# The opening phase of a one-core hybrid block: tokens turned by diagonal products, modulation weights loaded in groups, first projection weights kept

## The reference, cut to what matters

```python
mod_x = silu(c) @ w_ada + b_ada              # latent; six pieces of 1024 columns
mod_c = silu(c_ctx) @ w_ada + b_ada          # context
hx = rmsnorm(x, norm1_g) * (1 + sc1x) + sh1x
hc = rmsnorm(ctx, norm1_g) * (1 + sc1c) + sh1c
p  = h @ w_in                                # then two groups of mixers, merge, w_out, squared-ReLU MLP
```

## Time and profile before

| | us |
|---|---|
| median of 3 runs | 1781.2 |
| lowest and highest | 1779.32 and 1784.86 |
| profiled execution, its own time | 1786.23 |
| its span | 1784.4 |
| end of the last instruction of `modulate_phase` | 67.17 |
| first projection product | 74.98 |

### The profile page before, as it was taken

One profiled execution on the slowest core, in us unless ns is written; L12 is line 12 of the kernel. 1 busy time (PEld: TensorE's weight loads), 2 busy tenths in 40 slices (PEclk: granted clock), 3 DMA queues, 4 the chain that ended last, 5 costly groups with the idle time before them and its releaser, 6 DMA issues. The chain is left out here.

```text
span 1784.4 us, 35206 instructions
## 1 busy us (share of the span) xinstructions
PE 1579.5 (89%) x15022; PEld 1331.5 (75%) x15022; DVE 1015.5 (57%) x1542; ACT 640.9 (36%) x976; POOL 420.3 (24%) x369
## 2 busy tenths in 40 slices
PE   4599999999987878888876798799999989899997
PEld 1366887899987777777775687578888867787886
DVE  2534553101105777767676655845545588887975
ACT  3367436212112232222222323445545543233333
POOL 1301111111103555545544220422222200000000
PEclk7699999999998999989899899999999999999998
DMA  7213324336545433333322232044444487163422
GB/s 309 76 47 104 108 91 124 102 114 185 169 127 136 133 109 108 109 109 109 108 62 84 93 115 95 24 130 141 163 151 144 161 314 253 54 235 115 168 83 95
DMA packets 170269, 229.94 MB, mean 129 GB/s; under 512 B 34205, under 2 KB 102049, under 8 KB 169090
## 3 DMA queue, kind: packets, MB, share of 16 engines
q1 hardware_dynamic: 163602, 206.85, 35.9%
q0 software_dynamic: 6512, 20.84, 3.7%
HBM read 165.91 MB, written 61.73 MB: 128 GB/s over the span
## 5 line engine op out<-in xcount | busy, mean ns | idle before, releaser
L87 PE MATMUL fps<-xh_m,w1r_hi 128*128 128x512 f32 x448 | 177.5, 396 | 19.2 <-ACT s L2373 5.4
L87 PE MATMUL fps<-bh,ah 128*128 128x512 f32 x448 | 176.5, 394 | 14.3 <-DVE acc L2688 9.8
L88 PE MATMUL fps<-xl_m,w1r_hi 128*128 128x512 f32 x448 | 176.7, 394 | 0.0
L89 PE MATMUL fps<-xh_m,w1r_lo 128*128 128x512 f32 x448 | 176.4, 394 | 0.0
L89 PE MATMUL fps<-bh,al 128*128 128x512 f32 x448 | 175.7, 392 | 0.0
L88 PE MATMUL fps<-bl,ah 128*128 128x512 f32 x448 | 175.7, 392 | 0.0
L80 PE MATMUL ps_main<-hhi,whi 128*128 128x512 f32 (+3 forms) x360 | 137.0, 381 | 15.6 <-DVE wlo L694 11.7
L81 PE MATMUL ps_main<-hlo,whi 128*128 128x512 f32 (+3 forms) x360 | 133.5, 371 | 0.0
L82 PE MATMUL ps_main<-hhi,wlo 128*128 128x512 f32 (+3 forms) x360 | 133.4, 371 | 0.0
L2335 ACT ACTIVATE ah<-araw 128x2048 fp32r<-128x2048 f32 x28 | 53.7, 1918 | 186.0 <-PE fps L89 120.0
L80 PE MATMUL ps_main<-whi,hhi 128*128 128x256 f32 x416 | 120.2, 289 | 0.0
(11 more groups left out here) (304 smaller groups left out, 3575.0 us busy)
## 6 DMA issues: line engine op xcount, KB each, us to landing
s_hid<-hb SPq DMA_DIRECT2D x112, 256.0 KB, 2.3
araw<-s_hid SPq DMA_DIRECT2D x28, 1024.0 KB, 6.6
w1raw<-in_w_ff SPq DMA_DIRECT2D x16, 1024.0 KB, 6.2
w2b<-in_w_ff SPq DMA_DIRECT2D x16, 1024.0 KB, 6.9
raw<-in_w_in SPq DMA_DIRECT2D x14, 1024.0 KB, 5.3
wa<-in_w_ada SPq DMA_DIRECT2D x8, 1024.0 KB, 10.5
z_sb<-in_w_ada SPq DMA_DIRECT2D x16, 512.0 KB, 4.3
n_sb<-in_w_ada SPq DMA_DIRECT2D x16, 512.0 KB, 4.3
```

What stands on the lines that cost most here:

```text
L87: pe.matmul(out, lhi, rhi, start=start, stop=False, skip_group_check=True)
L88: pe.matmul(out, lhi, rlo, start=False, stop=False, skip_group_check=True)
L89: return pe.matmul(out, llo, rhi, start=False, stop=stop, skip_group_check=True)
```

## The change

In `modulate_phase`, a tile's `rstd` no longer multiplies the tokens. DVE multiplies the identity by it (a 128x128 diagonal, `diag`), and PE multiplies the token tile by this diagonal, an fp32 product that turns and scales at once, eight for a tile. What comes out is copied to `xt`, by DVE for tiles 0 to 5 and by ACT for 6 to 9. W_ada is loaded in five groups of feature columns (`GROUPS`: 2, 2, 2, 1 and 1 blocks of 128, shift and scale), the first between token tiles 5 and 6, the third to fifth into the memory of token tiles that have been turned. After each group comes a small chain of its own: `columns` (PE), `row` (ACT), `select` (PE), `scales` (DVE), and then for its feature blocks scale and shift in place (`full`, DVE or ACT), rounding (`high`, ACT) and subtraction (`low`, DVE) over 512 to 1280 tokens at a time. POOL has no part in it any more. The weights of "small" are loaded at the end of the phase's SP queue and split at the end of ACT's and DVE's, into tiles that both phases see (`K.ws_hi`, `K.ws_lo`). In `project_phase`, the "small" load and split are gone, the "k" weights are the first load, and the first product waits for nothing. Two small buffers move into the memory of others.

```diff
@@ modulate_phase @@
+        GROUPS = ((0, 2), (2, 2), (4, 2), (6, 1), (7, 1))
+        TOGETHER = ((0, 1), (1, 1), (2, 2), (4, 2), (6, 2), (8, 2))
+        xt = m.sb("xturn", [P, KT, NTOK])
+        junk = K.hhi[:, KT - 1, :D]
+        wa = m.sb("wa", [P, 2, 4 * D])
+        wslot = [x.rearrange("p (z k n) -> p z k n", z=2, k=KT) for x in
+                 (wa[:, 0], wa[:, 1], *(xs[:, a:b].rearrange("p t d -> p (t d)") for a, b in ((0, 4), (4, 6), (6, 8))))]
...
+        diag = K.gt2[:, 512:1024].rearrange("p (x n) -> p x n", n=P)
...
+        PIECES = [(0, 0, HALF), (1, 0, HALF), (0, HALF, NTOK), (1, HALF, NTOK), (2, 0, NTOK), (3, 0, NTOK), (4, 0, NTOK),
+                  (5, 0, NTOK), (6, 0, NTOK), (7, 0, HALF), (7, HALF, NTOK)]
+        BY_ACT = (1, 3, 5, 6)
+        T_ACT = 6
...
+            def load_w(g):
+                k, n = GROUPS[g]
+                for z in range(2):
+                    sp.dma_start(wslot[g][:, z], wv[:, z, :, k * P:(k + n) * P]).then_inc(ld_w[g][z], 16)
+
+            for t in range(4, 6):
+                sp.dma_start(xs[:, t], xr[t]).then_inc(ld_x[t], 16)
+            load_w(0)
+            for t in range(6, NT):
+                sp.dma_start(xs[:, t], xr[t]).then_inc(ld_x[t], 16)
+            load_w(1)
+            for g, last in ((2, 3), (3, 5), (4, 7)):
+                sp.wait_ge(t_ready, 2 * last + 2)
+                load_w(g)
+            wi = A["w_in"].rearrange("(k p) n -> p k n", p=P)
+            sp.wait_ge(wpad_done, 1)
+            sp.dma_start(wraw[:, :, 0:16], wi[:, :, OFF_R:OFF_R + 16]).then_inc(ld_small, 16)
+            sp.dma_start(wraw[:, :, 32:48], wi[:, :, OFF_AB:OFF_AB + 16]).then_inc(ld_small, 16)
...
+            def turned(t):
+                for h in range(2):
+                    act.wait_ge(t_ready, 2 * t + h + 1)
+                    act.activation(xt[:, features(h), tokens(t)], ps_t[:, 2 * (t % 2) + h].rearrange("p (k n) -> p k n", n=P),
+                                   ACT.Copy).then_inc(t_act, 1)
+
+            def row(g):
+                n = GROUPS[g][1]
+                act.wait_ge(w_used, g + 1)
+                if g:
+                    act.wait_ge(mod_ready, g)
+                act.activation(modrow[:, :2 * n * P], ps_row[:, :2 * n * P], ACT.Copy).then_inc(row_done, 1)
+
+            def full(x):
+                k, lo, hi = PIECES[x]
+                act.wait_ge(sc1_done, [k in range(a, a + n) for a, n in GROUPS].index(True) + 1)
+                if hi > HALF:
+                    act.wait_ge(t_act, 2 * (NT - T_ACT))
+                act.wait_ge(t_dve, 2 * T_ACT)
+                full_piece(act, lambda a, s, b: act.activation(a, a, ACT.Identity, scale=s, bias=b), x, hf_act)
+
+            def high(x):
+                k, lo, hi = PIECES[x]
+                act.wait_ge(hf_act if k in BY_ACT else hf_dve, fulls(x))
+                act.activation(K.hhi[:, k, lo:hi], xt[:, k, lo:hi], ACT.Copy).then_inc(hi_done, 1)
...
+                for t in range(t0, t0 + n):
+                    if t >= 4:
+                        dve.wait_ge(t_ready, 2 * (t - 3))
+                    dve.tensor_scalar(diag[:, t % 4], K.ident[:], rstd[:, t:t + 1], None, ALU.mult).then_inc(diag_done, 1)
+
+            def turned(t):
+                for h in range(2):
+                    dve.wait_ge(t_ready, 2 * t + h + 1)
+                    dve.tensor_copy(xt[:, features(h), tokens(t)],
+                                    ps_t[:, 2 * (t % 2) + h].rearrange("p (k n) -> p k n", n=P)).then_inc(t_dve, 1)
...
+            def turn(t):
+                pe.wait_ge(diag_done, t + 1)
+                if t >= 2:
+                    pe.wait_ge(t_dve, 2 * min(t - 1, T_ACT))
+                if t - 2 >= T_ACT:
+                    pe.wait_ge(t_act, 2 * (t - 1 - T_ACT))
+                for h in range(2):
+                    for i in range(4):
+                        k = 4 * h + i
+                        last = pe.matmul(ps_t[:, 2 * (t % 2) + h, i * P:(i + 1) * P], xs[:, t, k * P:(k + 1) * P],
+                                         diag[:, t % 4], start=True, stop=True)
+                    last.then_inc(t_ready, 1)
+
+            def columns(g):
+                n = GROUPS[g][1] * P
+                if g:
+                    pe.wait_ge(row_done, g)
+                for z in range(2):
+                    pe.wait_ge(ld_w[g][z], 16)
+                    for k in range(KT):
+                        q = slice(32 * (k % 4), 32 * (k % 4) + 32)
+                        last = pe.matmul(ps_row[q, z * n:(z + 1) * n], K.csil[:, k, :], wslot[g][:, z, k], start=(k < 4),
+                                         stop=(k >= 4))
+                last.then_inc(w_used, 1)
+
+            def select(g):
+                n = GROUPS[g][1]
+                pe.wait_ge(row_done, g + 1)
+                if g == 0:
+                    pe.wait_ge(sel_done, 1)
+                if g == 1:
+                    pe.wait_ge(cols_done, 1)
+                if g >= 2:
+                    pe.wait_ge(mod_done, g - 1)
+                for i in range(2 * n):
+                    last = pe.matmul(both[g % 2][:, 8 * g + 2 * i:8 * g + 2 * i + 2], modrow[:, i * P:(i + 1) * P], sel2[:],
+                                     start=True, stop=True)
+                last.then_inc(mod_ready, 1)
...
@@ project_phase, PE @@
-            pe.wait_ge(init_done, 3)
...
-                pe.wait_ge(lo_done, u + 1)
+                if u:
+                    pe.wait_ge(lo_done, u)
...
-                        last = mm3(pe, ps_main[:width, i % 3, :n], whi[:, b, k, :width], wlo[:, b, k, :width],
+                        last = mm3(pe, ps_main[:width, i % 3, :n], K.ws_hi[:, k], K.ws_lo[:, k],
```

More of the change, by code:

```diff
@@ new lines, in high, with roots @@
+            def high(x):
+                k, lo, hi = PIECES[x]
+                act.wait_ge(hf_act if k in BY_ACT else hf_dve, fulls(x))
+                act.activation(K.hhi[:, k, lo:hi], xt[:, k, lo:hi], ACT.Copy).then_inc(hi_done, 1)
+            def roots(r):
+                t, n = TOGETHER[r]
+                square(t)
+                if n == 2:
+                    square(t + 1)
+                rsqrt(r)
+            for r in range(5):
+                roots(r)
+            row(0)
+            roots(5)
@@ new lines, in _ @@
+            turned(6)
+            full(1)
+            turned(7)
+            high(0)
+            high(1)
+            turned(8)
+            turned(9)
+            full(3)
+            high(2)
+            high(3)
+            row(1)
+            full(5)
+            high(4)
+            high(5)
+            row(2)
+            full(7)
+            high(6)
+            high(7)
+            row(3)
+            full(8)
+            high(8)
+            act.wait_ge(ss_done, NT)
+            row(4)
@@ L202, in _ @@
+            high(9)
+            high(10)
+            act.wait_ge(ld_small, 32)
+            act.activation(K.ws_hi[:], wraw[:], ACT.Copy).then_inc(small_hi, 1)
         @block.vector
@@ L254, in _ @@
-            if on_dve(len(units) - 1):
-                low(len(units) - 1)
+            scales(0)
+            full(0)
+            variance(5)
+            diagonal(5)
+            low(0)
+            low(1)
+            full(2)
+            low(2)
+            low(3)
+            scales(1)
+            full(4)
+            low(4)
+            low(5)
+            scales(2)
+            full(6)
+            low(6)
+            low(7)
+            scales(3)
+            low(8)
+            scales(4)
@@ L283, in _ @@
[L283 to L296 removed]
+            columns(0)
@@ L299, in project_phase @@
+            select(0)
+            turn(6)
+            turn(7)
+            turn(8)
+            turn(9)
+            for g in range(1, NG):
+                columns(g)
+                select(g)
 def project_phase(nc, A, K, S):
```

278 lines of the change are left out of this document (124 added, 154 removed).

## The result

| | before | changed kernel |
|---|---|---|
| median | 1781.05 us (4 executions) | 1765.15 us (4 executions) |
| lowest and highest | 1779.32 and 1784.86 | 1763.3 and 1768.08 |
| profiled execution, its own time | 1786.23 | 1768.08 |
| its span | 1784.4 | 1766.3 |
| first projection product | 74.98 | 62.94 |

The ratio is 0.9906, with a 95% interval of 0.9884 to 0.9927. The direction was right, the size too small.

A forecast was written before the change was run, and what follows sets the result against it. PE's long run bounds the kernel, so its first product sets the end. The chain summed to a start at 66.1 against 74.98 us: gain 8.9, 1781.2 to 1772.3 us, range 1766.5 to 1780.5.

The forecast's parts named there:

- step 2: PE turns six token tiles by diagonal products: three half tiles at 2.01 us, nine at 1.09, ending at 23.7 us.
- steps 5 and 6: Group 1's columns at 1.2 GHz, to 40.8 us; then ACT-paced rounds of groups 1 to 3, to 60.0 us.
- steps 3 and 4: Group 0's columns, row and select, to 27.5 us; then turning four tiles at 8 x 1.09 us, to 36.2.
- rivals C and D: C (0.08): products never raise PE's clock, 1790.8 us. D (0.05): a later wait takes back the earlier start, about 1781.
- rival B: Chain losses: hand-overs 1.1 us, durations 3.9, clock falling at 30 us 4.6; time 1776 to 1781 us; chance 0.19.
- rival A: PE stays at or near 2.4 GHz to the phase's end: gain 12.1 us, time 1769 us; chance 0.18.
- Step 7: Tail of the first phase: last select, scales, full, high, low and small weights' split, ending at 65.1 us.

The follow-up runs named there:

- small weights kept alone: Kernel before, with only the small unit's weights loaded and split in its first phase, and the changed projection phase: median 1774.48 us, ratio 0.9969.
- new opening alone: Changed kernel with the small weights loaded and split behind the barrier again, as in the kernel before: median 1775.54 us, ratio 0.9964.
- changed, late start: Changed kernel with its first token load held back by ten POOL memsets: median 1777.57 us, ratio 0.9985.
- changed, second trace: Changed kernel run again without edits, beside the kernel before: median 1766.22 us, ratio 0.9912.
- rows early: Changed kernel with each group's ACT row moved ahead of the two roundings, and DVE's scales ahead of the second subtraction: median 1761.11 us, ratio 0.9895.
- tail on POOL: Kernel with rows early, plus one tail subtraction on POOL and the small weights' split in an earlier gap: median 1765.09 us, ratio 0.9911.
- small split in the gap: Kernel with rows early, plus the small weights' split in gaps of ACT and DVE, all subtractions on DVE: median 1762.71 us, ratio 0.9881.
- first group behind the tokens: Changed kernel with the first W_ada group loaded behind all ten token tiles: 1775.77 us, one execution.
- transposes: Changed kernel with plain transposes in place of the diagonal products, tokens not normalised by their own root: 1765.0 us, one execution.
- 24 filling products: Small split in the gap, plus unused PE products between columns and select of groups 1 to 4 and 24 behind the last select: 1762.05 us, ratio 0.9878.
- 14 filling products: Version with 24 filling products, with 14 instead of 24 behind the last select: median 1757.57 us, ratio 0.9878.

## Why the prediction was right, and where it was wrong

The forecast was 1772.3 us, and 1765.15 was measured. Of the 7.15 us between them, 3.2 are in the opening (first product at 62.94, not 66.1): the largest term is step 2, the price of the diagonal product, with 2.05 us, and next steps 5 and 6, with 1.9, where a low clock was taken for work that went at the high one (steps 3 and 4 were 0.8 us too short). The other 4 us are in no step, and their cause stays open.

**The bound and the barrier: right.** Whatever moves PE's first product moves the end. Against the gain by medians of the same sessions (two versions have one execution only):

| kernel | first product | earlier by | faster by | behind |
|---|---|---|---|---|
| small weights kept alone | 68.85 | 6.1 | 6.1 | 1711.3 |
| new opening alone | 67.34 | 7.6 | 5.1 | 1711.4 |
| changed, late start | 73.45 | 1.5 | 3.1 | 1699.1 |
| changed, first trace | 62.94 | 12.0 | 15.9 | 1703.4 |
| changed, second trace | 60.18 | 14.8 | 13.9 | 1703.9 |
| rows early | 58.09 | 16.9 | 19.5 | 1699.9 |
| tail on POOL | 60.07 | 14.9 | 15.0 | 1702.4 |
| small split in the gap | 60.31 | 14.7 | 18.9 | 1701.2 |
| first group behind the tokens (1) | 67.86 | 7.1 | 4.3 | 1706.1 |
| transposes (1) | 61.59 | 13.4 | 15.1 | 1701.6 |
| 24 filling products | 58.34 | 16.6 | 19.5 | 1701.0 |
| 14 filling products | 58.15 | 16.8 | 22.5 | 1697.7 |

The differences between the third and the fourth column go both ways, from -2.8 to +5.7 us; in the last two rows some 2 us are the faster small unit. One column is of one execution, the other a median of several. So rivals C and D are out: the start is kept, and the products raised the clock, as the window from 14 to 20 us shows (PE busy throughout, 1.00):

```profile
14.00:20.00 6.00, 6.00 (x55) 5.94 (x55) 4.88 (x11) 1.56 (x4) 0.00 (x0) 1.00 1.09 366
```

**Kept small weights: right.** 6.9 us of waiting behind the barrier were to go. From the phase's last instruction to the first product it is 7.9 us without the kept weights and 1.05 with them, 6.9 less.

**Step 2, the price of the diagonal product: wrong, and the largest error.** I took 2.01 and 1.09 us for half a tile from the earlier trace rows. The run of four tiles in the second trace, all at 2.4 GHz, gives 7.39/8 = 0.92 us for half a tile. The single records say it for both clocks: eight starts 0.213 us apart are 1.71 us at 1.2 GHz, eight 0.111 apart are 0.89 at 2.4. In the first trace the distance changes at 13.3 us, so 27 records of the first six tiles went at the one and 69 at the other: 5.8 + 7.7 = 13.4 us, and 0.5 us was spent where a run or a group begins. Together that is the measured 21.40 - 7.45 = 13.95 us. The forecast had 16.0, so the step was 2.05 us too long, of the 3.2 by which the first product was forecast too late. The earlier trace rows are differences between starts of two groups, and the single records of the same trace show what that adds: in the group at 540.56 the first two starts stand 0.38 us apart, the next ones 0.21, and 0.35 lie between the last and the group behind. That is 0.30 us in 2.01 which a long run pays once and not for each half tile; in the other group it is 0.20 in 1.09.

**Steps 3 and 4: too short by 0.8 us.** ACT's row came late for select 0 (1.51 us of wait in front of it; 4.36 us for the step, not 3.8), and the clock fell in step 4 (8.95, not 8.7), where with the clock up it would have been 7.3. In the second trace it was. This is rival B's falling clock in one execution and not in the other; it cost 1.6 us where B had 4.6.

**Steps 5 and 6: the clock did not fall at 36 us.** The granted clock was still up there, in the view of windows 1.00 from 36 to 40:

```profile
36.00:40.00 4.00, 1.84 (x24) 1.26 (x20) 2.25 (x4) 2.75 (x5) 0.00 (x0) 1.00 1.16 298
...
41.00:62.00 21.00, 9.24 (x96) 6.78 (x88) 13.00 (x21) 13.29 (x17) 0.00 (x0) 0.50 0.17 32
```

So the columns of group 1 took 1.93 us and not 3.86, and the second select 1.05 and not 1.88. Step 5 took 4.1 and not 4.6 us; it gained less than its columns because ACT's row stood only at 38.18, so ACT set the pace one step earlier than forecast. The rounds took 6.1, 6.7 and 5.1 us instead of 7.2, 6.95 and 5.05. This is the front half of rival A; the back half did not come, for from 41 to 62 us the clock was at 0.50 (second row). The form of the rounds was right: ACT sets the pace, with a gap ended by DVE's scales in each. Their `full` was dearer than the 1.47 us I took (1.73), the gaps up to 0.9 us shorter than 2.4 (1.5, 2.35, 1.8). **Step 7** was right: 5.3 us for 5.1.

With the chain's true length the forecast would have been 1781.2 - 12.0 = 1769.2, rival A's time, inside the range. **The last 4 us** are in no step. Behind the first product PE's instructions are the same in the two kernels (the order of a few loads differs), and still the four traces with the old opening or the old small unit have 1707.8 to 1711.4 us there, the ten others 1697.7 to 1706.1. Two things in the runs go with that. The four were taken of executions 3 to 7.4 us above the median of their kernel (that of the kept weights was the slowest of its twelve), and of the others the changed kernel's first was 2.9 us above, the rest 0.6 at most (two have a single execution). With that taken off, more than half of the difference is gone. And the clock stood at 1.2 GHz for 127 to 151 us behind the first product in the four, and for 111 to 126 in the ten; the spread is mostly between 600 and 1000 us. The first trace of before had 129, the changed kernel's 120: 9 us at half the clock are at most 5 us of work, an estimate. Why the clock was low for longer there no run shows. The late start, with the whole change in it, had 119.

Executions of the kernel before ran from 1772.88 to 1799.47 us with nothing changed. Over the 62 executions beside these experiments the mean is 1781.3, over the ten of the changed kernel 1766.1: 15.2 us, against 12.0 and 14.8 from the two traces' first products. What is left, some 2 us, these runs don't tell from the scatter, and whether there is a lasting part stays open. The forecast failed here in that its range had no term for this scatter: two medians of four executions drawn from those 62, whose standard deviation is 4.5 us, differ by 3 us or so without a cause in the code. That is an estimate.

The fastest versions are the three with early rows and the small split in the gap or with filling, 1757.6 to 1762.7 us, and the one with early rows alone at 1761.1. All have medians below the changed kernel's 1765.15 and 1766.22, but the intervals of their ratios overlap with its own. Which of them is best is not resolved.

## What to carry to other kernels

Where one engine runs almost without a gap behind a barrier, find its first instruction in the trace and measure changes ahead of it by that place: where the clock ahead of it was the same, it showed within one execution what eight executions blurred. Price a repeated instruction from a long run of its own kind (its time over the count of its records), not from the difference between starts of two short groups. And in a chain of engines, put what another engine waits for ahead of one's own long work; that was worth 2 us of path here for moving eight lines.

## What was unexpected of the hardware

The granted clock fell in the midst of work without a gap. In the version with 24 filling products PE was never idle from 50 to 57 us, and yet (columns as in the earlier trace rows):

```profile
50.00:51.00 1.00, 1.00 (x9) 1.00 (x10) 0.69 (x3) 0.70 (x1) 0.00 (x0) 0.91 0.00 0
51.00:54.40 3.40, 3.40 (x19) 3.40 (x18) 3.40 (x6) 1.48 (x2) 0.00 (x0) 0.52 0.00 0
54.40:57.00 2.60, 2.60 (x25) 2.60 (x25) 0.43 (x1) 0.00 (x0) 0.00 (x0) 1.00 0.00 0
```

Ahead of this fall PE had waited 1.4 us for ACT's row and then begun anew; ahead of the fall at 27.0 in the changed kernel it had waited 1.5 us, with 1.2 us of products since. In the second trace it had waited 0.9 us at that place, and the clock stayed. Over the traces with this opening, waits of 1.5 (twice), 1.7 and 2.15 us ahead of that select were followed by a fall, waits of 0.9, 1.2, 1.35, 1.6 and 1.9 us were not. So the length of that wait alone doesn't decide it. That the pause is the cause is likely, but not shown; what is shown is that the fall can come when the engine is already full again, and that it differs from one execution to the next, by 1.5 to 2.85 us at this place (8.87 to 10.24 against 7.39 us). Transposes brought the clock up too, but later: from a start at 7.5 to 8.0 us products had it up at 10.8 to 13.7, transposes in their one trace at 16.2. And beside a POOL instruction of 2.88 us one of DVE's smallest took 2.83.
